# A two-block transformer kernel: all of GpSimd's arithmetic moved to VectorE, attention head pairs visited in twos, rotary rows swapped by transfers

## The reference, cut to what matters

```python
# first block
h = rmsnorm(x, mix_norm);   proj = h @ w_in
x = x + concat(stick_breaking_attention(sq, sk, sv),      # 8 heads of 128
               gated_deltanet(gq, gk, gv, gz, gb, ga)) @ w_out
x = x + memory_cross_attention(rmsnorm(x, xattn_norm), rmsnorm(mem, mem_norm), w_xq, w_xkv, w_xo)
x = x + conv_ffn(rmsnorm(x, ffn_norm), w_up, ffn_conv, ffn_conv_bias, w_down)
x = rmsnorm(x, final_norm)
# second block
p = rmsnorm(x, n0) @ fox_w_in                             # 32 heads of 64
x = x + (fox_attention(q, k, v, log_f) * silu(gate)) @ fox_w_out
p = rmsnorm(x, n1) @ swa_w_in                             # 32 query heads, 4 key heads
q, k = partial_rope(q), partial_rope(k)                   # rows 0..15 of each head
x = x + (swa_attention(q, k, v, sinks) * silu(gate)) @ swa_w_out
out = rmsnorm(x, final_g_2)
```

## Time and profile before

| | |
|---|---|
| median of three runs | 2253.01 us |
| the profiled execution's own time | 2254.47 us |
| its span, first to last instruction | 2252.7 us |
| granted TensorE clock, mean | 0.996 of full speed |
| TensorE busy | 2216.2 us, 98% of the span |
| VectorE busy | 1644.7 us, 73% |
| ScalarE busy | 1315.0 us, 58% |
| GpSimd busy | 346.8 us, 15% |
| read from HBM | 383.10 MB, 171 GB/s over the span |

### The profile page before, as it was taken

How to read it: one execution, slowest core, us unless ns; L and a number is a source line. 1 busy time by engine, 2 the same in 40 slices (tenths; PEclk the granted TensorE clock), 3 DMA queues, 4 the chain that set the end, 5 groups by cost and what they waited for, 6 DMA issues and landing times.

```text
span 2252.7 us, 35286 instructions
## 1 busy us (share of the span) xinstructions
PE 2216.2 (98%) x13792; PEld 1907.6 (85%) x13792; DVE 1644.7 (73%) x2722; ACT 1315.0 (58%) x2507; POOL 346.8 (15%) x295
## 2 busy tenths in 40 slices
PE   7999999999999999999999999999999999999997
PEld 7878888888888888888888888888888888887886
DVE  7787655678778888755788867767676777777875
ACT  6855344775556666544666655555556655555654
POOL 1121201122111111000111101211110101232202
PEclk9999999999999999999999999999999999999999
DMA  6443233465545555555555555555544555433453
GB/s 240 168 139 115 104 117 118 156 246 187 172 156 188 187 187 189 195 187 189 189 192 187 187 185 191 195 178 178 184 172 158 184 182 192 166 130 131 140 197 122
DMA packets 106327, 387.54 MB, mean 172 GB/s; under 512 B 11808, under 2 KB 12064, under 8 KB 105520
## 3 DMA queue, kind: packets, MB, share of 16 engines
q1 hardware_dynamic: 104400, 376.85, 47.9%
q0 software_dynamic: 1760, 8.42, 1.0%
HBM read 383.10 MB, written 2.13 MB: 171 GB/s over the span
## 4 chain that ended last, share of the span: by engine, by line
PE 91%; DVE 5%; ACT 2%; issue 1%; POOL 1%; DMA 0%; SPq 0%; DVEq 0%; POOLq 0%; ACTq 0%
PE main L456 83%; PE ps L456 7%; DVE WL L857 1%; PE ps L459 1%; DVE A L863 1%; DVE M L863 1%; ACT WH L1395 0%; DVE XT L857 0%; ACT PPw L1395 0%; DMA RAW<-ws 0%; POOL PPw L1966 0%; DVE gt L857 0%; DVE GQ L863 0%; DVE PPw L857 0%; ACT A L1395 0%
## 5 line engine op out<-in xcount | busy, mean ns | idle before, releaser
L857 DVE TENSOR_TENSOR WL<-RAW,WH 128x512 fp32r<-128x512 f32 x1416 | 1065.3, 765 | 399.5 <-ACT WH L1395 389.3
L1395 ACT ACTIVATE WH<-RAW 128x512 fp32r<-128x512 f32 x1416 | 882.0, 629 | 660.7 <-PE main L456 653.9
L456 PE MATMUL main<-A,WH 128*128 128x512 f32 (+1 forms) x3680 | 1156.9, 397 | 15.5 <-DVE WL L857 12.3
L456 PEld LDWEIGHTS main<-A,WL 128*128 128x128 f32 x3584 | 676.6, 189 | 155.3
L456 PE MATMUL main<-A,WL 128*128 128x256 f32 x3584 | 716.3, 279 | 0.0
L456 PEld LDWEIGHTS main<-A,WH 128*128 128x128 f32 x3680 | 567.5, 190 | 38.5 <-DVE WL L857 17.1
L456 PE MATMUL main<-B,WH 128*128 128x512 f32 (+1 forms) x896 | 265.4, 380 | 2.7 <-DVE WL L857 2.7
L456 PE MATMUL main<-H,WH 128*128 128x512 f32 x704 | 221.1, 395 | 0.0
L456 PEld LDWEIGHTS main<-B,WL 128*128 128x128 f32 x832 | 156.5, 188 | 34.1
L456 PE MATMUL main<-B,WL 128*128 128x256 f32 x832 | 169.0, 278 | 0.0
L456 PEld LDWEIGHTS main<-H,WL 128*128 128x128 f32 x704 | 132.3, 188 | 31.3
(11 more groups left out here) (295 smaller groups left out, 1828.3 us busy)
## 6 DMA issues: line engine op xcount, KB each, us to landing
RAW<-ws SPq DMA_DIRECT2D x708, 512.0 KB, 3.3
CB<-cscr POOLq DMA_DIRECT2D x4, 1024.0 KB, 6.8
xs<-xT SPq DMA_DIRECT2D x8, 256.0 KB, 7.5
XT<-xT POOLq DMA_DIRECT2D x4, 512.0 KB, 7.4
MS<-memT POOLq DMA_DIRECT2D x4, 512.0 KB, 7.6
CST<-cst SPq DMA_DIRECT2D x1, 1056.0 KB, 7.6
out<-XT SPq DMA_DIRECT2D x2, 512.0 KB, 2.6
out<-XT SPq DMA_DIRECT2D x2, 256.0 KB, 2.1
```

Of the source, the lines that this page charges most:

```text
L456: return e.matmul(o, l, r, start=start, stop=True, skip_group_check=True)
L857: return e.tensor_tensor(o, a, b, op)
L1395: return e.activation(o, i, f, bias=bias, scale=scale, accum_out=accum)
```

## The change

GpSimd keeps its transfers and memsets and does no arithmetic. Its operations go to VectorE (`scale`, `add_squares`, `fold` and their callers); the scales run two ticks after a chunk's end. Masks that were affine selects become minima with constants (3.0e38 where a score stays, -1.0e30 or 0 where not). In SWA the minimum takes the place of the copy out of PSUM, of both heads, so ScalarE's copy of the first head goes. In `octet` the mask `below` is dropped; the other masks go to VectorE. For the first norm, ScalarE takes the squares of `x` after all its splits rather than between them, and the first chunk is evicted 4 ticks after its end.

Fox pairs now begin in twos every 22 ticks, and SWA pairs in twos every 10, with four lanes in place of three and scores, transposes and products of a pair in the same PSUM banks. Within a couple TensorE's three steps fall on the same tick. VectorE and ScalarE handle the second pair one or two ticks after the first.

Rope's rotation is four transfers of 8 rows each, per chunk, issued by SP between weight loads into `ROT`, which GpSimd clears once; the sign sits in the sine table. TensorE has no part in it, and the stream no wait for it.

```diff
-T_NORM = {0: 7, 1: END["wo3"] + 5, 2: END["xo3"] + 6, 4: END["fo3"] + 5}
+T_NORM = {0: 12, 1: END["wo3"] + 6, 2: END["xo3"] + 7, 4: END["fo3"] + 6}
...
-T_FOX = [[END[f"fv{g}"] + 2 + 11 * p for p in range(4)] for g in range(4)]
+T_FOX = [[END[f"fv{g}"] + 2 + 22 * (p // 2) for p in range(4)] for g in range(4)]
...
-T_SWA = [[END["wq0"] + 13 + 5 * (4 * g + p) for p in range(4)] for g in range(4)]
+T_WROPE = ENDS["wkv", 0] + 17
+T_QROPE = [[ENDS[f"wq{g}", p] + 10 for p in range(2)] for g in range(4)]
+T_SWA = [[END["wq0"] + 17 + 10 * (2 * g + p // 2) for p in range(4)] for g in range(4)]
...
-FOX_LANES, SWA_LANES = 2, 3
+FOX_LANES, SWA_LANES = 2, 4
+
+BEHIND = 2
...
+            def swap(r):
+
+                src, dst = wide_to(*ROPED[r]), ROT[r % 2]
+                w.wait_ge(s_scl, SCALED[ROPED[r]])
+                w.wait_ge(rp_zero, 1)
+                if r >= 2:
+                    w.wait_ge(rp_done, r - 1)
+                for base in (0, 64):
+                    lower, upper = slice(base, base + 8), slice(base + 8, base + 16)
+                    e.dma_start(dst[lower, :, :], src[upper, :, :]).then_inc(s_rot[r % 2], 16)
+                    e.dma_start(dst[upper, :, :], src[lower, :, :]).then_inc(s_rot[r % 2], 16)
+
             for i in range(RAHEAD, NS):
+                if i in ROT_AT:
+                    swap(ROT_AT[i])
                 load(i)
...
-                if i == 0 and (key, part) in ROPED:
-                    w.wait_ge(rp_done, ROPED[key, part])
...
-                yield from ticks(12)
+                yield from ticks(12 + BEHIND)
                 w.wait_ge(fp_ve[lane], F_VE * i + 3)
                 turn(PP[lane], two).then_inc(fp_pe[lane], 1)
...
-                yield from ticks(9)
+                yield from ticks(14)
+                if m < 14:
+
+                    w.wait_ge(wp_ve[(m + 2) % SWA_LANES], F_VE * ((m + 2) // SWA_LANES) + 1)
                 w.wait_ge(wp_ve[lane], F_VE * i + 3)
-                w.wait_ge(y_done, 16 + m)
-                turn(PPw[lane], banks[6:8]).then_inc(wp_pe[lane], 1)
+                turn(PPw[lane], two).then_inc(wp_pe[lane], 1)
...
+            def scale(key, part):
+
+                w.wait_ge(s_evac, CHUNK[key, part] + 1)
...
+                d, rb = wide_to(key, part), bm((RBm if key == "xk" else RB)[:], 2)
+                tt(d, d, rb, ALU.mult).then_inc(s_scl, 1)
+
+            def add_squares(stage, n):
+                if n:
+                    w.wait_ge(s_sq, SQN[stage] + n + 1)
+                    w.wait_ge(s_acc, ACN[stage] + n - 1)
+                    tt(ACC[:], ACC[:], SQ[:], ALU.add).then_inc(s_acc, 1)
...
+                w.wait_ge(v_own, t)
+                tt(S[:, :, 0:128], S[:, :, 0:128], bm(K["low"], 2), ALU.min)
+                tt(S[:, :, 256:384], S[:, :, 256:384], bm(K["low"], 2), ALU.min).then_inc(fp_ve[lane], 1)
...
-                e.tensor_copy(S[:, 1, :], banks[5][:, 0:384]).then_inc(wp_ve[lane], 1)
+                tt(S[:, 0, :], banks[4 + 2 * (m % 2)][:, 0:384], band, ALU.min)
+                tt(S[:, 1, :], bank[:, 0:384], band, ALU.min).then_inc(wp_ve[lane], 1)
...
+                w.wait_ge(s_rot[r % 2], 64 * (r // 2 + 1))
+                v, d = ROT[r % 2][:], wide_to(key, part)
+                tt(d, d, bm(ROPC, 2), ALU.mult)
                 t = own(tt(v, v, bm(ROPS, 2), ALU.mult))
...
-            for k0, k1 in ((5, 9), (9, 12), (12, 14)):
+            for k0, k1 in ((0, 4), (4, 8), (8, 12), (12, 14)):
                 tt(XT[:, k0:k1, :], XT[:, k0:k1, :], bm(RB[:], k1 - k0), ALU.mult).then_inc(fin_ve, 1)
```

More of the change, by code:

```diff
@@ L528, in norm @@
                 b = banks[7] if i != 2 else banks[4]
[L529 removed]
+                yield from ticks(3)
                 w.wait_ge(s_cst, 16)
@@ L966, in evac, with fold, sums, x_sums @@
                 z.then_inc(fin_ve if key == "w23" else s_evac, 1)
+            def scale(key, part):
+                w.wait_ge(s_evac, CHUNK[key, part] + 1)
+                if key == "xk":
+                    w.wait_ge(s_mrb, 1)
+                else:
+                    w.wait_ge(s_rb, 2 if key == "xq" else 3 if key[:2] in ("fg", "fu") else {"f": 4, "w": 5}.get(key[0], 1))
+                d, rb = wide_to(key, part), bm((RBm if key == "xk" else RB)[:], 2)
[5 more added lines that the diff above has]
+                    tt(ACC[:], ACC[:], SQ[:], ALU.add).then_inc(s_acc, 1)
+            def fold(acc):
+                z = tt(acc[:, 0:2, :], acc[:, 0:2, :], acc[:, 2:4, :], ALU.add)
+                w.wait_ge(v_own, own(z))
+                return tt(acc[:, 0, :], acc[:, 0, :], acc[:, 1, :], ALU.add)
+            def sums(stage, n):
+                add_squares(stage, n)
+                yield
+            def x_sums():
+                for n in range(1, 4):
+                    add_squares("x", n)
+                    yield from ticks(2)
             def x_split(kt):
@@ L1082, in octet @@
                 tt(t3, bm(K["eye"], 8), t2, ALU.subtract).then_inc(qd_ve, 1)
-                yield from ticks(2)
+                yield
+                for b in range(2):
+                    q = GQ[:, h4, 128 * b:128 * b + 128]
+                    tt(q, q, t7[:, b], ALU.mult).then_inc(qd_mu, 1)
+                yield
                 for b, o in enumerate((X, Z)):
@@ L1153, in mem @@
                     lo_of(ML, MH, kt, MS[:, kt, :], gain["mem_norm"][:, kt:kt + 1]).then_inc(s_M, 1)
+                    if kt in (8, 12):
+                        add(kt // 4 - 1)
                     yield
-                yield from ticks(12)
+                add(3)
+                yield
+                w.wait_ge(s_macc, 3)
+                fold(ACM).then_inc(s_mfold, 1)
+                yield from ticks(11)
                 w.wait_ge(s_mtr, 1)
@@ L1651, in dnorm @@
             def dnorm():
-                yield from ticks(10)
+                yield from ticks(4)
                 w.wait_ge(dn_pe, 1)
@@ L1721, in keys @@
             def keys():
-                yield from ticks(3)
+                yield from ticks(5)
                 w.wait_ge(rp_done, 1)
@@ L2001, in program @@
+            parts += [(END["gz1"], reload()), (T_MEM, mem()), (T_FF, forget())]
+            parts += [(END[f"fv{g}"], bias(g)) for g in range(4)] + [(END["fo0"], clear())]
+            interleave(parts, NH, lambda j: None)
         block = ctx.enter_context(nc.Block())
```

366 lines of the change are left out of this document (138 added, 228 removed).

## The result

The changed kernel takes 2217.35 us (median of 4 runs, 2216.93 to 2217.46), the kernel before 2253.5 in the same session (2252.32 to 2254.28): a ratio of 0.984, with a 95% interval of 0.9823 to 0.9857, or 36 us less. The profiled execution took 2217.3 us with a span of 2215.5.

The account below looks back on a forecast made before the run. TensorE was taken as the bound, busy 2216.2 of 2252.7 us. Terms summed to 31.0, with about 2 for small SWA waits 33: 2254.5 - 33 = 2221.5, so 2220 for the median; range 2209 to 2240.

Parts of the forecast that it names:

- Start: First norm's squares, adds and fold off GpSimd: TensorE's early waits and lower clock go, 6.0 us gained, bounds 3 and 6.5.
- Delta rule: GpSimd's operations in each `octet` go to VectorE: first group's wait and clock loss shrink, 3.2 us gained, bounds 0 and 4.3.
- `mem`: While `mem` is split, TensorE's wait of 1.80 falls to a few tenths: 1.5 us gained, bounds 0 and 1.8.
- Third norm: Waits of 0.92 and 1.51 and 1.6 of clock at stake: 3.5 us gained, bounds 1 and 4.
- Scales elsewhere: Scales in all other stages move to VectorE: 0 gained where TensorE never waited, cost covered by VectorE's four-half lead.
- Rope: Nine rope visits of TensorE go, 0.87 us each: 7.5 us gained, bounds 5 and 8; SP's transfers are hidden, 0.
- Visits in twos: Joining pairs' visits saves 0.6 us for each of 8 fox and 8 SWA couples: 9.6, bounds 6.5 and 12.
- the rival that a visit's cost lies within it: Joining TensorE's visits for pairs gains nothing, and the time is 2230 us; chance 0.12.
- VectorE in SWA: VectorE comes level with TensorE in three rope stretches: 1.5 us lost. Rival, VectorE pacing SWA: 2242 us median, chance 0.12.
- Small waits in SWA: About 2 us gained from SWA waits under 0.9 us that are not in the rows.
- VectorE stops for the couples: Slower case: VectorE's lead is used up at the couples' copies and TensorE stands: median 2264 us, chance 0.08.
- End: VectorE's last scalings, done alone, take 4.9 us instead of 6.1: 1.2 us gained, bounds 0.5 and 1.3.

Follow-up runs that it names:

- second experiment: The changed kernel with all scales and the norms' sums and folds back on GpSimd, in their new order and ticks: 2231.45 us, ratio 0.99.
- fourth run: The changed kernel with only the 44 scales of the FFN chunks back on GpSimd: 2217.97 us, ratio 0.9841.
- seventh experiment: The changed kernel with SWA's masks back on GpSimd as three affine selects per pair, VectorE's two minima becoming copies: 2219.71 us, ratio 0.9844.

## Why the prediction was right, and where its terms were off

The forecast was 2220.0 and the time is 2217.35, inside the range; its mechanism held in the main and none of its rivals did. The terms come to 33.0 where the traces differ by 37.2; the medians are closer (36.2), because the profiled run of before lay 1.0 above its median. So the terms are short by 4.2, more than the 2.65 by which the forecast missed. One sum is wrong: all upper bounds together, with the 2 for small waits, give 39.9 and not 44, so the lowest time by them was 2213 and not 2209. And the 0.42 that was held against the stretched splits is an addition's; a split takes 0.48. By its steps:

- **Start (6.0, measured 6.6).** Right in size. With the adds back on GpSimd 4.5 to 5.3 are lost, with the old order alone none, so taking them from GpSimd is what gained. That they worked by holding VectorE up is read from the trace of before; in the second experiment TensorE waits for GpSimd's own fold instead.
- **Delta rule (3.2, measured 3.0).** Right in size. The waits are 1.2 shorter and the lower clock is gone. Its products bring back 1.9; the rest, with the mask `below` that is no longer made, wasn't tried alone.
- **`mem` (1.5, measured 3.8).** The term that was mis-sized. The step took the single wait of 1.80 from rows 6 and bounded the whole by it. The trace of before has two more there, of 0.27 and 0.66, under the 0.9 us from which the rows were chosen. Most of the other 1.1 lies in the halves beside the waits: the half with the wait of 1.80 takes 3.35 us, 0.16 more than 1.39 and the wait, and the half behind each wait takes 1.50 for 1.39. Undone, 4.2 come back, but 1.7 of them by a clock that falls only then; the wait of 0.66 doesn't return, so 1.3 of the gain is not shown by any experiment. The bound (0 to 1.8) should have come from the stage's length against its matmuls.
- **Third norm (3.5, measured 4.5).** Over its upper bound of 4. With sums and scales on GpSimd both waits return and 2.9 us with them; the other 1.6 are the lower clock behind them (1.6 by rows 3), which that run didn't have.
- **Scales elsewhere (0).** Right where TensorE waits for nothing: shown in the FFN by the fourth run, where the four halves of lead cover it.
- **Rope (7.5).** The visits cost 0.85 to 0.87 each, as step 5 had it. The 32 transfers for the queries kept nobody waiting: no wait of TensorE in SWA names them.
- **Visits in twos (0.6 per couple).** Right per couple (0.56), and in its parts: 0.2 behind and 0.1 within, transposes nothing. This rules out the rival that a visit's cost lies within it.
- **VectorE in SWA (-1.5).** Measured 1.4, as two waits. VectorE comes level with TensorE and doesn't pace it: that rival wanted 9 us lost. Because of these waits the two steps before don't add up: undone one at a time, pairs lose 1.4 and rope 1.9 less than their matmuls cost.
- **Small waits in SWA (2).** Right in size. The trace of before has four, of 0.32, 0.40, 0.70 and 1.00, 2.4 in all, and none is left. Two end with work on `AQ`, rope's tile, and two with ScalarE's copies of the transposed weights:

```profile
2047.84 0.70 PE L456 MATMUL main<-A,WH 128*128 128x512 f32 x2 [0.70 <-DVE AQ L857]
...
2123.30 0.88 PE L456 MATMUL ps<-PTw,WV 128*64 128x256 f32 x8 [1.00 <-ACT PTw L1395]
```

No run shows which part of the change took the last two away. The 2.6 lost with the masks on GpSimd come by other waits (0.66, 1.09, 1.46), in a kernel whose VectorE is short of time there, so they don't measure this term. SWA's sum: 7.7 + 4.5 + 2.4 - 1.4 = 13.2 of the 14.0 gained.
- **VectorE stops for the couples (the slower case).** Behind the copies no wait for the remainders but two, of 0.44 and 0.30 at 1743 and 1748 us, at the last couple, which shares VectorE with the gates. The 2.5 us to spare were enough elsewhere.
- **End (1.2, measured 0.9).** VectorE's scalings run from 2207.33 to 2212.23, 4.90 us where 4.9 was worked out, 1.2 less than before; the last transfer took 0.2 more. In two edited kernels that don't differ there the end took another 0.9 more, so a gain of this size is not clear of the scatter between single executions:

```profile
2207.33 4.10 DVE L881 TENSOR_TENSOR XT<-XT,RB 128x1024 f32<-128x1024 f32 x4 [2.84 <-ACT RB L1508]
...
2211.35 0.88 DVE L887 SCALAR_TENSOR_TENSOR XT<-XT,PAR,RB 128x256 f32<-128x256 f32 x2
```

The Trainium skill (SBUF — State Buffer, "SBUF: two separate sides") says that of a VectorE instruction with two inputs in SBUF and a GpSimd instruction that reads SBUF, the one that starts first has the port pair that they share for its whole length, and the other waits. The traces agree both ways: the split that began 0.04 us behind the add of 2.42 ended 0.3 behind it, and the selects of the seventh experiment that began during a VectorE operation ended 0.27 behind that one, whether it had 0.45 or 0.58 to go.

## What to carry to other kernels

Before giving work to GpSimd, look at VectorE's longest instruction of a kind against its median: where they part by a GpSimd operation's length, VectorE pays more for the help than the work costs. It matters only where VectorE has no lead over TensorE. In this kernel small matmuls between a stream's cost 0.2 us behind them when they use half the array, so join those and leave the full-sized ones where they are. Bound a stage's gain by its length against its matmuls, not by its longest wait: at `mem` the one wait of 1.80 stood for 3.8 us.

## What was not expected of the hardware

- Visits of 128*128 matmuls leave the stream's pace alone (8 behind them in 1.41 us), those of 64*128 and 128*64 cost it 0.2 (1.59): 12 visits joined at the stick-breaking heads saved nothing.
- Beside GpSimd only VectorE's operations with two operands in SBUF were held up: a split beside an add of 2.42 took 2.2 us longer and an operation beside a select 0.21, but copies out of PSUM and row maxima kept their length. GpSimd is held up as well: a select of 0.40 took up to 0.85 behind VectorE.
- The same waits don't always bring the same clock: after 0.91 and 1.53 at the third norm it stayed at 1.00 in one run and fell to 0.59 in the kernel before; after 1.8 at `mem` it was the other way round, 0.68 and 1.00.
- The first matmul began between 7.6 and 9.1 us, and from the last chunk's start to the end it took 24.2 or 25.1, in kernels that don't differ there. A difference of 1 us between single executions of this kernel has to be read by stage.
